# Router, second tile's transposes, gather and second gate's rows rearranged in a two-block transformer kernel

## The chip, the core and the metric

The kernel runs on one core of a Trainium2 chip. The core has TensorE (PE, matrix products into PSUM), VectorE (DVE), ScalarE (ACT), GpSimd (POOL) and SyncE (SP, which issues nearly all DMAs here). Each engine has its own instruction queue, and they meet only at semaphores. The metric is the device time of one execution in microseconds, the median over runs. A profiled execution gives one trace; its times are counted from the start of the span.

## What is computed

Two transformer blocks over 256 tokens of width 1024, all in float32. The first mixes tokens in two branches, normalises, and then sends each token to 4 of 32 experts. Only that part is touched by the change, together with the last gate of the second block:

```
h = layer_norm(ALPHA * x + mix, ln1_g, ln1_b)
logits = h @ router_w + router_b
top_vals, top_idx = lax.top_k(logits, 4)
gates = softmax(top_vals)
# for each chosen expert e of a token:
hcat = h @ w_up[e] + b_up[e]                  # 1024 x 2048
act = glu(hcat)                               # clipped, sigmoid(1.702 * x) gate
y_e = act @ w_down[e] + b_down[e]             # 1024 x 1024
out = sum over chosen e of gates[e] * y_e
# second block, at its end:
x = x + g1 * (mixed @ w_out)
x = x + g2 * ((silu(gt) * up) @ w_down)
```

`g1` and `g2` are rows of 1024 numbers that come out of `c @ w_ada`; every token uses the same row.

## The kernel before

The program is a row of blocks, `first_mix`, `branches`, `experts`, `second_mix`, `output`. Within a block each engine has a list of instructions in the order in which the code is written, and between blocks all engines meet at a barrier. The tokens are two tiles (t = 0, 1) of 128.

**Routing, the end of `branches`.** VectorE normalises a tile in two halves of 512 columns (L1125, L1127). TensorE turns each half (`turn`, L925, four transposes of 128x128 into one PSUM bank), ScalarE or VectorE copies it out to `hT` (tile name `fbuf_sgq`), and TensorE multiplies by the router's weights (`logits`, L936). Then for each tile VectorE's `top` adds the bias, takes the eight largest, finds their indices, converts these, compares them with 0..31 and sums the one-hots to `chosen` (L1132 to L1138). ScalarE takes the exponentials. TensorE adds up `chosen` over tokens (L993 to L997), which gives each token its place in each expert's list and the count of each expert. VectorE makes the gates (L1155 to L1158), the places (L1162, L1164) and, by `choose` (L860), the one-hot `sel` (tile name `keep_tri`) that picks up to 64 tokens for each of the first two experts. A `fill` is a matmul whose result nobody reads. `gate_rows` (L942) spreads g1 and g2 over all partitions by a product of ones with a diagonal matrix; ScalarE copies them to `gB`, which lies over the diagonals.

**Experts.** Each engine enters the block after the barrier. SyncE issues the load of the down biases (L1253, into `y`), reads the number of extra rounds that VectorE works out from the counts, and goes on to refill chunks. TensorE waits for `sel`, gathers the chosen tokens (L870, 32 matmul instructions), reads the rounds (L1244), waits for both bias loads (L1298, `bias_in`), enters two nested loops (L1366, L1367) and starts a pair of experts after a wait for `xg_ready`, which ScalarE gives after copying the gathered rows to `xg`. A pair is two experts in 12 chunks of 2 MB: up-weights (L1307), down-weights (L1332), transposes, a scatter-add (L1291), and the gather for the next pair. There are 16 pairs. VectorE chooses for the next pair inside the loop.

**Weights.** Nine chunks fit into memory. SyncE issues all nine during `branches`, as the space comes free, the last two (into `more`) after the last product with `w_out`. From then on each further chunk waits until TensorE has used one up:

```
for i in range(lo, hi):
    sp.wait_ge(used, done + 2 * (i - PLACES + 1))
    load_expert(k, sp, a, first, i)
```

`used` counts up by one for every 8 matmul instructions of weights, so the first refill waits for 16. All loads by SyncE go through one queue.

**Output block.** TensorE runs three fills (L2100) while VectorE normalises, then transposes and multiplies by `w_out`, `w_gu` and `w_down`; the last step on VectorE multiplies by g2 (L2317).

## Time and profile before

| | us |
|---|---|
| median of three runs | 1532.1 |
| lowest, highest run | 1530.8, 1532.8 |
| the profiled execution | 1531.5 |
| its span | 1529.6 |

| engine | busy us | share of the span |
|---|---|---|
| TensorE, matmuls | 1423.6 | 93% |
| TensorE, weight loads | 838.8 | 55% |
| VectorE | 591.9 | 39% |
| ScalarE | 444.9 | 29% |
| GpSimd | 39.1 | 3% |

The DMA engines moved 516 MB, on average 338 GB/s. A busy TensorE is not yet an engine at its limit: matmuls are pipelined and their ends are modelled. An idle time in a timeline stands in brackets, with what ended it. A wait for several semaphores is put down to the engine that came last. "issue" means that nothing the profile shows was waited for, and an engine's name with a q means its sequencer, which runs register steps, waits and branches. The granted clock (PEclk) is a share of 2.4 GHz.

### The profile page before, as it was taken

What the parts mean: (1) busy time and instruction counts of PE and PEld (TensorE: products, weight loads), DVE (VectorE), ACT (ScalarE), POOL (GpSimd) and SP (SyncE); (2) the same over time, 40 slices, a digit from 0 to 9 for tenths busy, and PEclk for the clock granted to TensorE, in tenths of its full rate; (3) what the DMA queues carried; (4) which work ended last, traced back from release to release, by engine and by line L of the source; (5) the groups of instructions that cost most, each with busy time, mean ns of one, the idle gap of its engine ahead of it and who ended that gap; (6) DMA issues with size and microseconds to landing.
All of it is one profiled execution on the core that took longest, in us unless ns stands there. A gap on an engine that the chain in (4) does not pass through costs nothing. (4 is left out here: it accounts for less than half of the span.)

```text
span 1529.6 us, 19821 instructions
## 1 busy us (share of the span) xinstructions
PE 1423.6 (93%) x7981; PEld 838.8 (55%) x7981; DVE 591.9 (39%) x1030; ACT 444.9 (29%) x577; POOL 39.1 (3%) x80
## 2 busy tenths in 40 slices
PE   8999999999999999988988988989988999899998
PEld 8988798344334434323423423323333788788887
DVE  4985447211210211210210210210211786677765
ACT  5654533121111112111111111111111536454343
POOL 2000030000000000000000000000000022000000
PEclk9999999999999999999999999999999999999999
DMA  9598999899999999999999999999999361345552
GB/s 283 171 299 272 327 334 397 361 426 429 427 428 428 428 428 428 429 428 428 429 428 429 428 429 428 429 428 429 428 427 382 104 191 56 99 150 193 192 187 88
DMA packets 126901, 516.46 MB, mean 338 GB/s; under 512 B 6869, under 2 KB 95294, under 8 KB 102238
## 3 DMA queue, kind: packets, MB, share of 16 engines
q1 hardware_dynamic: 126558, 514.64, 84.6%
q10 hardware_dynamic: 288, 1.05, 0.2%
q8 instruction: 39, 0.64, 0.2%
q14 instruction: 16, 0.13, 0.0%
HBM read 514.62 MB, written 1.05 MB: 337 GB/s over the span
## 5 line engine op out<-in xcount | busy, mean ns | idle before, releaser
L1307 PE MATMUL ps<-ring,xg 128*64 128x512 f32 x1456 | 324.8, 595 | 27.3 <-DMA ring<-in_expert_w_up 23.2
L1450 DVE TENSOR_TENSOR glu<-ps,bupT 128x512 f32<-128x512 f32 x32 | 22.1, 692 | 717.5 <-PE ps L1316 717.5
L1307 PEld LDWEIGHTS ps<-ring,xg 128*64 128x64 f32 x1456 | 101.7, 137 | 244.8 <-issue 186.2
L86 ACT ACTIVATE hrow<-ps 128x1024 f32<-128x1024 f32 x32 | 32.7, 1023 | 474.4 <-PE ps L1307 474.4
L1332 PE MATMUL ps<-ring,act 128*64 128x512 f32 x608 | 136.8, 597 | 1.2 <-ACT y L86 1.1
L2134 PE MATMUL ps<-h_halves,w_hi 128*128 128x512 f32 x352 | 123.1, 394 | 1.1 <-DVE h_halves L2287 1.1
L2236 DVE TENSOR_TENSOR w_lo<-ring,w_hi 128x2048 fp32r<-128x2048 f32 x36 | 82.5, 2291 | 61.2 <-ACT w_hi L86 61.2
L1307 PE MATMUL ps<-more,xg 128*64 128x512 f32 x416 | 93.1, 595 | 8.4 <-DMA more<-in_expert_w_up 7.2
L2136 PE MATMUL ps<-h_halves,w_lo 128*128 128x256 f32 x352 | 98.7, 280 | 0.0
L86 ACT ACTIVATE y<-ps 64x512 f32<-64x512 f32 x64 | 37.8, 591 | 182.8 <-PE ps L1332 182.5
L86 ACT ACTIVATE w_hi<-ring 128x2048 fp32r<-128x2048 f32 (+1 forms) x38 | 70.7, 1864 | 60.0 <-PE ps L2136 32.6
L86 ACT ACTIVATE in_hi<-ring 128x1024 fp32r<-128x1024 f32 (+1 forms) x72 | 72.4, 1043 | 52.2 <-DMA ring<-in_w_in 24.7
L1332 PEld LDWEIGHTS ps<-ring,act 128*64 128x64 f32 x608 | 41.5, 137 | 82.3 <-issue 72.5
L270 DVE TENSOR_TENSOR in_lo<-ring,in_hi 128x1024 fp32r<-128x1024 f32 x56 | 66.2, 1220 | 49.7 <-ACT in_hi L86 49.7
L538 PE MATMUL ps<-x_hi,in_hi 128*128 128x256 f32 x272 | 77.8, 286 | 0.0
L538 PE MATMUL ps<-x_lo,in_hi 128*128 128x256 f32 x272 | 76.0, 279 | 0.0
L538 PE MATMUL ps<-x_hi,in_lo 128*128 128x256 f32 x272 | 75.9, 279 | 0.0
L2134 PEld LDWEIGHTS ps<-h_halves,w_hi 128*128 128x128 f32 x352 | 66.0, 187 | 16.6 <-issue 1.3
L1316 PE MATMUL ps<-ident,hrow 128*128 128x128 f32 x256 | 36.5, 286 | 37.4 <-ACT hrow L86 37.4
L870 PE MATMUL ps<-keep_tri,h 128*128 128x128 f32 x544 | 67.3, 282 | 0.6 <-PEq L898 0.6
L1307 PEld LDWEIGHTS ps<-more,xg 128*64 128x64 f32 x416 | 28.9, 137 | 70.9 <-issue 51.8
L870 PEld LDWEIGHTS ps<-keep_tri,h 128*128 128x128 f32 x544 | 65.5, 196 | 3.0 <-issue 1.6
(409 smaller groups left out, 2218.1 us busy)
## 6 DMA issues: line engine op xcount, KB each, us to landing
ring<-in_expert_w_up SPq DMA_DIRECT2D x91, 2048.0 KB, 36.8
ring<-in_expert_w_down SPq DMA_DIRECT2D x38, 2048.0 KB, 39.3
more<-in_expert_w_up SPq DMA_DIRECT2D x26, 2048.0 KB, 35.5
more<-in_expert_w_down SPq DMA_DIRECT2D x16, 2048.0 KB, 38.8
ring<-in_w_in SPq DMA_DIRECT2D x29, 1024.0 KB, 9.0
ring<-in_w_ada SPq DMA_DIRECT2D x24, 1024.0 KB, 6.5
x_xT_xn<-in_expert_w_up SPq DMA_DIRECT2D x11, 2048.0 KB, 36.9
ring<-in_w_gu SPq DMA_DIRECT2D x22, 1024.0 KB, 5.1
```

Of the source, the lines that this page charges most:

```text
L86: return nc.scalar.activation(out, x, ACT.Copy)
L270: nc.vector.tensor_tensor(k.wlo1[:, n % 4, :], w[:, half * 1024:(half + 1) * 1024], k.whi1[:, n % 4, :].bitcast(F32), ALU.subtract).then_i ...
L538: last = nc.tensor.matmul(out, left, right, start=(j == 0 and kq == 0 and m == 0), stop=(j == 1 and kq == KD - 1 and m == 2), skip_group_c ...
L870: last = nc.tensor.matmul(out, k.h[:, t, (q // 2) * 256 + q % 2:(q // 2 + 1) * 256:2], k.sel[:, t, :], start=(t == 0), stop=(t == TT - 1))
L1307: last = nc.tensor.matmul(up[a2 * CAP:(a2 + 1) * CAP, u, :], k.xg[:, q, h * CAP:(h + 1) * CAP], w[:, c:c + 512], start=(q == 0), stop=(q = ...
L1316: last = nc.tensor.transpose(turned[:, par, j * P:(j + 1) * P], k.hrow[:, hidden_columns(j, par)], k.ident[:, :])
L1332: last = nc.tensor.matmul(down[a2 * CAP:(a2 + 1) * CAP, :], k.act[:, h, m % 4, m // 4, :], w[:, c:c + 512], start=(m == 0), stop=(m == KF ...
L1450: link(nc.vector.tensor_tensor(k.glu[:, :, :, :], g, b[:, 0].to_broadcast(wide), ALU.add))
L2134: nc.tensor.matmul(out, w[0][:, q, s], k.hh[:, q, :, :].rearrange("p v t -> p (v t)"), start=(i == 0), stop=False, skip_group_check=True)
L2136: last = nc.tensor.matmul(out[:, 0:T], w[1][:, q, s], k.hhi[:, q, :], start=False, stop=(i == KD - 1), skip_group_check=True)
L2236: nc.vector.tensor_tensor(k.wlo[i % 2][:, :], k.ring[:, LATE[i % len(LATE)], :], k.whi[i % 2][:, :].bitcast(F32), ALU.subtract).then_inc(w ...
```

## The change

The changes, in the order of the program:

- The slot numbers count from 1 (`iota`), so that a place is (position + 1) * chosen and 0 where a token isn't chosen; the subtraction of 1 goes.
- The second tile's transposes go half by half into two banks each. ScalarE copies the first two blocks of 128 of each half and VectorE the other two. The logits of the second tile are summed in pairs of blocks, the first of them before the tile's last transposes.
- `top`: the logits get four columns of 3e38 behind the 32, so the eight largest hold these four and the four chosen ones; a match-and-replace takes the eight out, and `chosen` is where something changed. The negated maximum, which ScalarE waits for, comes last.
- The rows of g1 are made in two parts, one between the tiles and one behind. The rows of g2 are made in the output block, in place of two of three fills, and ScalarE copies them there; TensorE waits for that copy before the third chunk of `w_out`.
- The counts of the experts go to a bank of their own, with a second `pos_done`, which VectorE waits for in the next block.
- `choose` without gates is one compare of 256 elements in place of four of 64, also inside the expert loop.
- The first half of the first gather stands in the routing block, in place of its last fill. All gathers are signalled by halves, ScalarE copies `xg` in halves, and the up-weights of a pair wait for the first half before block 0 and for the second before block 4.

The bias load, its wait and the places where the chunks are issued are as before.

TensorE, from the end of the routing block to the first expert's matmuls, before. `keep_tri` is `sel`, `ring` holds weights.

```order
L878 MATMUL ps<-h,ident 128x512
L898 UNCONDITIONAL_BRANCH
L1286 UNCONDITIONAL_BRANCH [waits barrier_Pool_Activation_PE_DVE_SP_release]
L870 MATMUL ps<-keep_tri,h 128x128 [waits hot_ready]
L870 MATMUL ps<-keep_tri,h 128x128 x15
L1244 TENSOR_LOAD rounds [waits rounds]
L1244 ISA x2
L1366 UNCONDITIONAL_BRANCH [waits bias_in]
L1367 UNCONDITIONAL_BRANCH
L1367 ISA
L1193 ISA [waits xg_ready]
```

The same place in the change:

```order
L875 MATMUL ps<-keep_tri,h 128x128 [waits hot_ready]
L875 MATMUL ps<-keep_tri,h 128x128 x7
L904 UNCONDITIONAL_BRANCH
L1290 UNCONDITIONAL_BRANCH [waits barrier_Pool_Activation_PE_DVE_SP_release]
L875 MATMUL ps<-keep_tri,h 128x128 x8
L1248 TENSOR_LOAD rounds [waits rounds]
L1248 ISA x2
L1371 UNCONDITIONAL_BRANCH [waits bias_in]
L1372 UNCONDITIONAL_BRANCH
L1372 ISA
L1197 ISA [waits xg_ready]
L1312 MATMUL ps<-ring,xg 64x512 [waits expert_in0]
```

Half of the gather now stands ahead of the barrier and the fill is gone; rounds, `bias_in`, loop entry and `xg_ready` follow in the same order.

VectorE, `top` of one tile, before (`m` is the eight largest, `ada_acc` the one-hot):

```order
L1132 TENSOR_TENSOR lg<-ps,rb 128x32 [waits logits_done]
L1133 MAX m<-lg 128x8 [waits chain_dve]
L1134 TENSOR_SCALAR small<-m 128x1 [waits chain_dve]
L1135 MAX_INDEX ix<-m,lg 128x8
L1136 CAST ixf<-ix 128x8 [waits chain_dve]
L1137 TENSOR_TENSOR ada_acc<-iota,ixf 128x128 [waits chain_dve]
L1138 TENSOR_REDUCE chosen<-ada_acc 128x32 [waits chain_dve]
```

and in the change:

```order
L1137 TENSOR_TENSOR lg<-ps,rb 128x32 [waits logits_done]
L1138 MAX m<-lg 128x8 [waits chain_dve]
L1139 MATCH_REPLACE rest_lg<-m,lg 128x36 [waits chain_dve]
L1140 TENSOR_TENSOR chosen<-rest_lg,lg 128x32 [waits chain_dve]
L1142 TENSOR_SCALAR small<-m 128x1
```

Seven instructions have become five. VectorE, from the positions to `sel`, before:

```order
L1162 SCALAR_TENSOR_TENSOR place<-ps,chosen 128x2x32 [waits pos_done]
L1164 TENSOR_SCALAR place<-place 128x2x32 [waits chain_dve]
L860 TENSOR_SCALAR keep_tri<-iota,place 128x64 [waits chain_dve]
```

and in the change:

```order
L1167 SCALAR_TENSOR_TENSOR place<-ps,chosen 128x2x32 [waits pos_done]
L859 TENSOR_TENSOR keep_tri<-iota,place 128x256 [waits chain_dve]
```

The subtraction and three of four compares (the row `x3` behind these) are gone.

The core of the diff:

```diff
-            link(nc.gpsimd.iota(k.iota_i[:, :], pattern=[[1, CAP]], base=0, channel_multiplier=0))
+            link(nc.gpsimd.iota(k.iota_i[:, :], pattern=[[1, CAP]], base=1, channel_multiplier=0))
...
+    if not gated:
+        both = [P, TT, 2, CAP]
+        return nc.vector.tensor_tensor(k.sel.rearrange("p t (h n) -> p t h n", h=2),
+                                       k.slots[:, :].unsqueeze(1).unsqueeze(1).to_broadcast(both),
+                                       k.place[:, :, bass.ds(p * 2, 2)].unsqueeze(3).to_broadcast(both), ALU.is_equal)
     for h in range(2):
         for t in range(TT):
             place = k.place[:, t, bass.ds(p * 2 + h, 1)]
-            g = (k.gate[:, t, bass.ds(p * 2 + h, 1)], ALU.mult) if gated else (None, ALU.bypass)
-            last = nc.vector.tensor_scalar((k.sel_gated if gated else k.sel)[:, t, h * CAP:(h + 1) * CAP], k.slots[:, :],
-                                           place, g[0], ALU.is_equal, g[1])
+            last = nc.vector.tensor_scalar(k.sel_gated[:, t, h * CAP:(h + 1) * CAP], k.slots[:, :], place,
+                                           k.gate[:, t, bass.ds(p * 2 + h, 1)], ALU.is_equal, ALU.mult)
...
-                    last = nc.tensor.transpose(k.ps[:, bank[t][half], j * P:(j + 1) * P],
+                    b, at = (bank[t][half], j) if t == 0 else (bank[t][half] + 4 * (j // 2), j % 2)
+                    last = nc.tensor.transpose(k.ps[:, b, at * P:(at + 1) * P],
...
-            logits(0)
-            gate_rows(0)
+            logits(0, range(4)).then_inc(log_done, 1)
+            gate_row(0)
             turn(1, 0)
+            logits(1, (0,))
             turn(1, 1)
-            logits(1)
-            gate_rows(1)
+            logits(1, (1, 2, 3)).then_inc(log_done, 1)
+            gate_row(1).then_inc(gb_done, 1)
             pe.wait_ge(m_ready, 2)
             mm = k.chosen
             nc.tensor.matmul(k.ps[:, 4, 0:E], k.strict[:, :], mm[:, 0, :], start=True, stop=True)
             nc.tensor.matmul(k.ps[:, 4, E:2 * E], k.ones[:, :], mm[:, 0, :], start=True, stop=False)
-            nc.tensor.matmul(k.ps[:, 4, E:2 * E], k.strict[:, :], mm[:, 1, :], start=False, stop=True)
-            nc.tensor.matmul(k.ps[:, 4, 2 * E:3 * E], k.ones[:, :], mm[:, 0, :], start=True, stop=False)
-            nc.tensor.matmul(k.ps[:, 4, 2 * E:3 * E], k.ones[:, :], mm[:, 1, :], start=False, stop=True)\
+            nc.tensor.matmul(k.ps[:, 4, E:2 * E], k.strict[:, :], mm[:, 1, :], start=False, stop=True)\
+                .then_inc(pos_done, 1)
+            nc.tensor.matmul(k.ps[:, 7, 0:E], k.ones[:, :], mm[:, 0, :], start=True, stop=False)
+            nc.tensor.matmul(k.ps[:, 7, 0:E], k.ones[:, :], mm[:, 1, :], start=False, stop=True)\
                 .then_inc(pos_done, 1)
             pe.wait_ge(gate_ready, 1)
             for t in range(TT):
-                last = nc.tensor.transpose(k.ps[0:E, 5, t * P:(t + 1) * P], k.gate[:, t, :], k.ident[:, :])
+                last = nc.tensor.transpose(k.ps[0:E, 6, t * P:(t + 1) * P], k.gate[:, t, :], k.ident[:, :])
             last.then_inc(gT_done, 1)
-            fill(nc, k, 3, k.h[:, 0, 0:512], 1)
+            pe.wait_ge(k.hot_ready, 1)
+            gather(nc, k, 5, range(4)).then_inc(k.g_done, 1)
...
-                if t == 0:
-                    evacuate(0, 1)
+                evacuate(t, 1)
             for t in range(TT):
                 act.wait_ge(negmax, t + 1)
-                nc.scalar.activation(ex[:, t, :], lg[:, t, :], ACT.Exp, bias=k.small[:, t:t + 1]).then_inc(expd, 1)
-            for n in range(2):
-                gate_copy(n)
+                nc.scalar.activation(ex[:, t, :], lg[:, t, 0:E], ACT.Exp, bias=k.small[:, t:t + 1]).then_inc(expd, 1)
+            act.wait_ge(gb_done, 1)
+            act_copy(nc, k.gB[:, 0, :], k.flat[:, 0:1024])
...
+            link(nc.vector.memset(lg[:, :, E:E + 4], LARGE))
...
-                link(nc.vector.tensor_tensor(lg[:, t, :], k.ps[:, 4 + t, 0:E], k.rb[:, :], ALU.add))
+                link(nc.vector.tensor_tensor(lg[:, t, 0:E], k.ps[:, 4 + t, 0:E], k.rb[:, :], ALU.add))
                 link(nc.vector.max(m8[:, t, :], lg[:, t, :]))
-                nc.vector.tensor_scalar(k.small[:, t:t + 1], m8[:, t, 0:1], -1.0, None, ALU.mult).then_inc(negmax, 1)
-                link(nc.vector.max_index(ix[:, t, :], m8[:, t, :], lg[:, t, :]))
-                link(nc.vector.tensor_copy(ixf[:, t, :], ix[:, t, :]))
-                link(nc.vector.tensor_tensor(one_hot[:, t], bc(k.iota[:, 0:E], 1, 4), bc(ixf[:, t, 0:4], 2, E), ALU.is_equal))
-                nc.vector.tensor_reduce(k.chosen[:, t, :], one_hot[:, t].rearrange("p j e -> p e j"), AX.X, ALU.add)\
+                link(nc.vector.match_replace(rest_lg[:, t, :], m8[:, t, :], lg[:, t, :], -LARGE))
+                nc.vector.tensor_tensor(k.chosen[:, t, :], rest_lg[:, t, 0:E], lg[:, t, 0:E], ALU.not_equal)\
                     .then_inc(m_ready, 1)
+                nc.vector.tensor_scalar(k.small[:, t:t + 1], m8[:, t, 4:5], -1.0, None, ALU.mult).then_inc(negmax, 1)
...
-            dve.wait_ge(hT_done, 4)
-            nc.vector.tensor_copy(hT[:, 4:8, P:T], k.ps[:, bank[1][1], :].rearrange("p (k n) -> p k n", k=4))\
-                .then_inc(hT_last, 1)
+            for half in range(2):
+                dve.wait_ge(hT_done, half + 3)
+                nc.vector.tensor_copy(hT[:, 4 * half + 2:4 * half + 4, P:T],
+                                      k.ps[:, bank[1][half] + 4, 0:2 * P].rearrange("p (k n) -> p k n", k=2))\
+                    .then_inc(hT_last, 1)
...
-            link(nc.vector.tensor_scalar(pl, pl, -1.0, None, ALU.add))
...
-            pe.wait_ge(hot_ready, 1)
-            gather(nc, k, 5, range(KD)).then_inc(g_done, 1)
+            gather(nc, k, 5, range(4, KD)).then_inc(g_done, 1)
             extra = extra_rounds(pe)
             pe.wait_ge(k.bias_in, 32)
             def up_weights(r, turn, at, n, h):
                 for q in range(KD):
+                    if h == 0 and q % 4 == 0:
+                        pe.wait_ge(xg_ready, n * 2 + q // 4 + 1)
...
-                pe.wait_ge(xg_ready, n + 1)
...
-                    gather(nc, k, 5, range(KD)).then_inc(g_done, 1)
+                    for half in range(2):
+                        gather(nc, k, 5, range(4 * half, 4 * half + 4)).then_inc(g_done, 1)
...
-            act.wait_ge(g_done, 1)
-            act_copy(nc, k.xg[:, :, :].rearrange("p k n -> p (k n)"), flat(rows)).then_inc(xg_ready, 1)
+            def gathered(n, src):
+                for half in range(2):
+                    act.wait_ge(g_done, n * 2 + half + 1)
+                    act_copy(nc, k.xg[:, 4 * half:4 * half + 4, :].rearrange("p k n -> p (k n)"), src[:, half, :])\
+                        .then_inc(xg_ready, 1)
+
+            gathered(0, rows)
...
+            dve.wait_ge(k.pos_done, 2)
+            start(nc.vector.tensor_reduce(k.small[:, 8:9], k.ps[:, 7, 0:E], AX.X, ALU.max))
...
-            fill(nc, k, 4, k.gB[:, 0, 0:512], 3)
+            for half in range(2):
+                last = nc.tensor.matmul(k.ps[:, 6 + half, :], k.ones[:, :], k.diag[1][:, half * 512:(half + 1) * 512],
+                                        start=True, stop=True)
+            last.then_inc(k.gb_done, 1)
+            fill(nc, k, 4, k.gB[:, 0, 0:512], 1)
             turned(mixed, mn, mt)
             for c in range(4):
                 w = chunk(L_OUT + c)
+                if c == 2:
+                    pe.wait_ge(g2_copied, 1)
...
+            act.wait_ge(k.gb_done, 2)
+            act_copy(nc, k.gB[:, 1, :], k.flat[:, 3072:4096]).then_inc(g2_copied, 1)
```

## Rows read from the trace of the kernel before

**Rows 1.** The page, the span in 40 slices: busy share of the DMA engines, tenths.
```profile
DMA  9598999899999999999999999999999361345552
```

**Rows 2.** Waits of TensorE, 300 to 1180 us: waiter, releaser: us, times, longest.
```profile
PE ps L1307 <- DMA ring<-in_expert_w_up: 23.2, 19, 1.2
```

**Rows 3.** Busy time by window: us, five engines with counts, PEclk, DMA share, GB/s.
```profile
266.00:267.00 1.00, 0.28 (x3) 0.09 (x1) 0.82 (x2) 0.69 (x1) 0.00 (x0) 1.00 0.09 29
267.00:272.50 5.50, 4.69 (x22) 1.69 (x24) 0.00 (x0) 3.16 (x4) 0.00 (x0) 1.00 0.00 0
...
276.00:1170.00 894.00, 817.52 (x3912) 321.98 (x3910) 173.98 (x353) 148.24 (x186) 0.00 (x0) 1.00 1.01 428
```

**Rows 4.** Timeline of SyncE's DMA issues: start, duration, line, transfer.
```profile
249.65 0.43 SPq L1218 DMA_DIRECT2D more<-in_expert_w_down  x1
262.22 0.33 SPq L1253 DMA_DIRECT2D y<-in_expert_b_down  x1
271.67 7.17 SPq L1218 DMA_DIRECT2D ring<-in_expert_w_down  x3
```

**Rows 5.** Timeline of TensorE, end of routing: start, duration, [idle before <-releaser].
```profile
259.32 0.41 PE L993 MATMUL ps<-chosen,strict 128*128 128x32 f32 x2 [0.21 <-DVE chosen L1138]
...
262.27 4.01 PE L870 MATMUL ps<-keep_tri,h 128*128 128x128 f32 x32 [0.57 <-PEq L898]
267.81 13.95 PE L1307 MATMUL ps<-ring,xg 128*64 128x512 f32 x64 [1.53 <-ACT xg L86]
```

**Rows 6.** Timeline of ScalarE: the copy of the gathered rows.
```profile
266.31 1.02 ACT L86 ACTIVATE xg<-ps 128x1024 f32<-128x1024 f32 x1 [5.07 <-PE ps L870]
```

**Rows 7.** Instructions of TensorE's sequencer by line: duration ns, first, last start.
```profile
L1244 PEldq SEQ_ASSERT  x1: 32/32/32, 264.8 to 264.8; - x1
...
L1366 PEldq MOVE  x2: 29/36/42, 267.2 to 267.2; - x2
...
L1193 PEldq FUSED_REGOPS  x1: 102/102/102, 267.6 to 267.6; - x1
```

**Rows 8.** Load into `y` (down biases): issue to landing.
```profile
DMA to landing us min/median/max: 4.9/4.9/4.9
```

**Rows 9.** Loads into `more`, issued at 249.28 and 249.65: issue to landing.
```profile
DMA to landing us min/median/max: 12.3/14.8/17.2
```

**Rows 10.** Timeline of VectorE: last copy, router, place, one-hot.
```profile
255.32 0.69 DVE L1149 COPY fbuf_sgq<-ps 128x512 f32<-128x512 f32 x1 [0.75 <-PE ps L925]
255.92 0.18 DVE L1132 TENSOR_TENSOR lg<-ps,rb 128x32 f32<-128x32 f32 x1
...
258.56 0.29 DVE L1137 TENSOR_TENSOR ada_acc<-iota,ixf 128x128 f32<-128x128 f32 x1
258.89 0.37 DVE L1138 TENSOR_REDUCE chosen<-ada_acc 128x32 f32<-128x128 f32 x1
...
260.66 0.23 DVE L1162 SCALAR_TENSOR_TENSOR place<-ps,chosen 128x64 f32<-128x64 f32 x1 [0.42 <-PE ps L997]
...
261.15 0.74 DVE L860 TENSOR_SCALAR keep_tri<-iota,place 128x64 f32<-128x64 f32 x4
```

**Rows 11.** Timelines of TensorE and ScalarE, start of the output block.
```profile
1302.93 2.81 PE L878 MATMUL ps<-x_xT_xn,ident 128*128 128x512 f32 x6 [1.50 <-PEq L1517]
...
1317.83 0.42 ACT L2196 ACTIVATE x_xT_xn<-h 128x256 f32<-128x256 f32 x1 [5.88 <-DVE h L2270]
```

**Rows 12.** Timeline of TensorE, start of the program.
```profile
8.76 1.97 PE L548 MATMUL ps<-ident,x_xT_xn 128*128 128x128 f32 x8 [2.20 <-DMA x_xT_xn<-in_x]
...
12.23 1.91 PE L518 MATMUL ps<-x_hi,in_lo 128*128 128x256 f32 x8
13.94 1.16 PE L518 MATMUL ps<-x_lo,in_hi 128*128 128x256 f32 x8
```

**Rows 13.** Busy time by window, end of the program; columns as in rows 3.
```profile
1525.70:1529.50 3.80, 0.07 (x1) 0.00 (x0) 1.49 (x3) 0.00 (x0) 0.00 (x0) 1.00 0.46 176
1529.50:1529.60 0.10, 0.00 (x0) 0.00 (x0) 0.00 (x0) 0.00 (x0) 0.00 (x0) 0.80 0.00 0
```

66 lines of the change are left out of this document (29 added, 37 removed).

## The prediction

> **What bounds the kernel now.** I read the slices of the page first. The DMA line is 9 in nearly every slice from about 270 us to 1170 us [rows 1]: this is the expert stage, which streams every expert's weights. The list of what TensorE waited for in that stage has the stream in it: 23.2 us in 19 waits for up-weights in the ring [rows 2]. The windows say how full the stream is: from 276 to 1170 us the 16 DMA engines are busy (1.01) at 428 GB/s, and from 267.0 to 272.5 us they do nothing at all [rows 3]. So the stage ends when a fixed number of bytes has passed, and it can end earlier only if the hole of 5.5 us in front of the stream gets smaller. TensorE's waits for weights show that it keeps nothing in reserve by the end, so I take one microsecond at the first refill as one microsecond at the end.
>
> What ends the hole? SyncE issued the last of the nine chunks that fit before the stage at 249.65, then the small load of the down biases at 262.22, and the first refill only at 271.67 [rows 4]. The refill waits until TensorE has used up one chunk, that is 16 matmuls into the expert loop, and the loop's first matmul began at 267.81 [rows 5]. So the question for this change is one only: **what let TensorE start at 267.81?**
>
> The obvious answer is the routing chain: choice, positions, one-hot, gather, then ScalarE's copy `xg`, from 266.31 for 1.02 us, so done at 267.33 [rows 6]. The sequencer's own rows say something else [rows 7]. It finished reading the number of rounds at 264.8 (SEQ_ASSERT, L1244). Its next instruction is the loop entry of L1366, which stands behind the wait for `bias_in` at L1298, and it ran at 267.2. Two more steps follow, and the register step of L1193, which carries the wait for `xg_ready`, ran at 267.6, about 0.3 us after `xg` was finished. The down biases were issued at 262.22 and landed 4.9 us later [rows 4, 8], at 267.12. That fits the 267.2. **TensorE waited for the bias load, not for routing.** `xg` came second, with 0.3 us to spare.
>
> Why 4.9 us for 128 KB? The load stands in SyncE's queue behind the chunk issued at 249.65, which landed 17.2 us after its issue [rows 4, 9], at 266.85. The biases are done 0.27 us after the data in front of them. Issuing them a little earlier or later would change nothing.
>
> **The change part by part.** The sum is made against the profiled execution, 1531.5 us (span 1529.6 and 1.9 around it), which lies 0.6 below the median 1532.1 of the three runs.
>
> *Second tile in two banks.* VectorE's copy of 512 columns took 0.69 us [rows 10]. It becomes two of 256 columns, one of them before the last transposes. Half a copy is about 0.42 with the fixed part, so the chain gets 0.25 shorter. One of the two gate-row pairs of matmuls also no longer stands before the second tile's transposes. But VectorE delivers that tile's second half only at 254.57 anyway (it then waits 0.75 for the transposes, [rows 10]), so I count nothing.
>
> *Router in fewer operations.* From the end of the copy (255.92) to the end of the second `chosen` (258.89 + 0.37) were 3.3 us for two tiles [rows 10], 1.63 each. The index search, cast, one-hot of 128 elements (0.29) and reduction (0.37) go. A match-and-replace and a compare over 32 elements come; the trace has no match-and-replace. Bounds: as cheap as a small operation (0.2) or as dear as the one-hot and reduction that it replaces (0.7). I take 0.3, since it reads as few elements as the index search. About 0.95 per tile is left, so `chosen` is ready 1.4 us earlier, with the copies 1.65.
>
> *Positions.* TensorE does six matmul instructions instead of ten before the first `pos_done`, the stretch from 259.32 on [rows 5], about 0.5 less. VectorE is still busy with the four gate operations then, so the place step, at 260.66 now, moves by 1.6 and not by 2.1.
>
> *Place and one-hot.* From the place step at 260.66 to the first compare at 261.15 are two small operations; the subtraction, half of that, goes (0.25). Four compares, 0.74 together, become one of 256 elements. It lies between 0.29 (128 elements) and 0.69 (512), at 0.42 [rows 10]. Together 0.5 us. `hot_ready` then comes at about 259.75 instead of 261.9.
>
> *Gather by halves.* The first 16 of 32 matmuls, about 2.0 of the 4.01 us [rows 5], run before the blocks change, from 259.85 to 261.85. All engines meet at the block's end, so TensorE's half sets that point, at about 262.1; it was 262.2. The second half ends near 264.2 (now 266.28), and the second half copy of `xg` near 264.9 (now 267.33). **Routing and gather are 2.1 to 2.4 us shorter.**
>
> *What is left of it at the start of the experts.* The order on TensorE is gather, rounds, `bias_in`, loop entry, `xg_ready`; the diff does not touch the wait or the load. The load is issued at 262.1 instead of 262.2 and still lies behind the chunks that land at 266.85. It lands at 267.1, and the loop begins 0.65 later, at 267.8: **0.0**. The 2.4 us turn into waiting. The cover works both ways: routing may be 2.3 us dearer than I think before it costs anything.
>
> *Inside the loop.* ScalarE copies `xg` twice (about 0.6 each) instead of once (1.02), VectorE makes one compare instead of four, TensorE has one more wait. The copy is needed one stretch of down-weights later, and the stage is held by the stream [rows 3]: 0. If that cover were gone it would be 0.2 us in each of 16 pairs, 3 us.
>
> *Second gate's rows.* TensorE replaces two of the three fill matmuls of the output block by the two gate-row matmuls of the same 512 columns [rows 11]. ScalarE gets a copy of 1.02 us there and has 5.88 us idle right behind it [rows 11]: 0. In the routing block its removed copy was off the path: 0.
>
> Sum: 0.0, from -0.3 to +0.3 for the spread of the landing. **Forecast 1532.1**, no difference that can be measured.
>
> **The rivals.** *The clock drops.* TensorE's idle time before the expert loop was 1.53 us [rows 5]. It becomes 267.8 - 264.25 = 3.55 us, since the gather ends earlier, the start does not, and the fill at the block's end is gone. The longest between two matmuls in this trace is 2.20 us, near its start [rows 12]; the 1.53 us left the clock at 1.00 [rows 3]. At the very end the granted clock fell (mean 0.80 in the last 0.1 us) some 3.8 us after the last matmul [rows 13]. 3.55 is less than 3.8, but not by much. Price: at the start of the program eight matmuls of 256 columns took 1.91 us at 12.23 and 1.16 at 13.94 [rows 12], so the lower of the two levels, 1.2 GHz, held for some 5.2 us from the restart at 8.76. The 16 matmuls up to the first refill take 3.45 us at 2.4 GHz (a quarter of the 13.95 for 64, [rows 5]). At half clock 12 of them fill the 5.2 us and 4 follow at full clock: 6.1, so 2.6 later, **1534.7**; if all 16 are slow 3.4, 1535.5. It decides once the idle time is long enough, and nothing gives it back, since the stream starts later. The Trainium skill, page TensorE: Matmul & The Clock Gate, section Why this matters for your kernels, advises against idle gaps of this kind, because the gate then returns to half clock. By that rule this case, with the 1534.7 worked out above, would be the one to expect; no idle time within this trace is long enough to agree or not.
>
> *The biases land earlier.* If the 4.9 us are a matter of issue and not of the queue in front, TensorE starts when `xg` is ready, at 265.2 instead of 267.8: **1529.5**. Against it speaks that both landings lie 0.27 apart [rows 8, 9]. The Trainium skill, page DMA: Bandwidth & Descriptors, gives a fixed cost of about 2 us to a transfer; by that the load would land at some 264.4, and the trace's 4.9 speaks for the queue.
>
> *The change doesn't do what it says.* If routing were over 2.3 us dearer (a match-and-replace or a wide compare of several us), the start would slip by the rest. No row is near that: about 1533.
>
> **How the numbers follow.** Forecast 0.70, clock 0.17, earlier landing 0.08, dearer routing or something unseen 0.05. The three runs spread from 1530.8 to 1532.8, so the forecast alone spans 1530.7 to 1533.5. The range reaches to 1535.0 for most of the clock case, and to 1530.2 below; the earlier landing is left out. A difference of 0.2%, 3.1 us, is about what a measurement can tell. Only the case of 16 slow matmuls passes it upwards (1535.5), which with the unseen gives slower 0.10. The earlier landing stays just within it (1529.5 is 0.17%), so faster has 0.07 and same 0.83.
>
> **What would show it.** Right: the gather's second half ends near 264.2; the loop entry runs at 267.2 again, straight after the biases' landing; the first expert matmul is at 267.8 and the first refill at 271.7; TensorE's idle time before it is about 3.5 us; the DMA hole is still 5.5 us. Wrong: a loop entry well before 267 (earlier landing), a granted clock under 1.00 behind 265 with the refill at 274 (clock), or a place step no earlier than 260.7 (routing).

## The result: slower, and most of it before the changed code begins

The two kernels, timed beside each other:

| | before | after |
|---|---|---|
| median of 8 executions each, us | 1533.0 (1530.8 to 1534.4) | 1536.1 (1535.1 to 1539.9) |
| ratio, 95% interval | | 1.0027 [1.0016, 1.0038] |
| span of the profiled execution, us | 1529.6 | 1533.3 |
| mean granted clock in it | 1.000 | 0.998 |

Forecast: 1532.1, no measurable difference, range up to 1535.0. The changed kernel is slower, by 3.1 us in the medians and by 4.1 us by the ratio. A second comparison (after_again, below) gave 1.0040 [1.0027, 1.0053]. All of this is far under 2%; "slower" means here that the interval lies above 1.

The timeline of TensorE in the changed kernel: the end of the first stage, routing, the entry to the expert loop. Columns as in [rows 5].

```profile
251.51 0.28 PE L973 MATMUL ps<-in_hi,x_lo 128*128 128x256 f32 x1
251.63 1.04 PE L932 MATMUL ps<-ident,h 128*128 128x128 f32 x8
...
262.59 2.15 PE L875 MATMUL ps<-keep_tri,h 128*128 128x128 f32 x16 [0.20 <-DVE keep_tri L859]
265.07 2.12 PE L875 MATMUL ps<-keep_tri,h 128*128 128x128 f32 x16 [0.33 <-PEq L904]
269.80 6.64 PE L1312 MATMUL ps<-ring,xg 128*64 128x512 f32 x22 [2.61 <-DMA y<-in_expert_b_down]
```

And the two rows of the kernel before that answer to the first two:

```profile
248.97 0.28 PE L968 MATMUL ps<-in_hi,x_lo 128*128 128x256 f32 x1
249.09 0.38 PE L925 MATMUL ps<-ident,h 128*128 128x128 f32 x2
```

Three things stand in these rows. **The transposes that begin the routing block start 2.54 us late** (251.63 against 249.09), and everything ahead of them is code that the diff leaves alone. **The expert loop starts 2.0 us late** (269.80 against 267.81 in [rows 5]), so routing gained something, and its idle time is now put down to the bias load. **That idle time is 2.61 us, against 1.53.**

VectorE in routing, with the new operations:

```profile
257.02 0.42 DVE L1153 COPY fbuf_sgq<-ps 128x256 f32<-128x256 f32 x1
257.99 0.42 DVE L1153 COPY fbuf_sgq<-ps 128x256 f32<-128x256 f32 x1 [0.54 <-PE ps L932]
258.33 0.18 DVE L1137 TENSOR_TENSOR lg<-ps,rb 128x32 f32<-128x32 f32 x1
...
258.85 0.18 DVE L1139 MATCH_REPLACE8 rest_lg<-m,lg 128x36 f32<-128x36 f32 x1
259.07 0.19 DVE L1140 TENSOR_TENSOR chosen<-rest_lg,lg 128x32 f32<-128x32 f32 x1
...
261.00 0.22 DVE L1160 TENSOR_TENSOR ex<-ex,chosen 128x64 f32<-128x64 f32 x1 [0.46 <-ACT ex L1044]
...
261.86 0.22 DVE L1167 SCALAR_TENSOR_TENSOR place<-ps,chosen 128x64 f32<-128x64 f32 x1
262.11 0.43 DVE L859 TENSOR_TENSOR keep_tri<-iota,place 128x256 f32<-128x256 f32 x1
```

The match-and-replace takes 0.18 us, the wide compare 0.43. A new wait of 0.46 for ScalarE's exponentials stands ahead of the gate operations; the faster choice has caught up with them.

SyncE's issues, and how long the two loads ahead of the expert loop took from issue to landing (`y`, then `more`):

```profile
252.20 0.43 SPq L1222 DMA_DIRECT2D more<-in_expert_w_down  x1
265.01 0.33 SPq L1257 DMA_DIRECT2D y<-in_expert_b_down  x1
275.36 7.17 SPq L1222 DMA_DIRECT2D ring<-in_expert_w_down  x3
```
```profile
DMA to landing us min/median/max: 4.1/4.1/4.1
```
```profile
DMA to landing us min/median/max: 11.6/14.2/16.7
```

Biases: 265.01 + 4.1 = 269.11. The last chunk in front of them: 252.20 + 16.7 = 268.90. The loop entry of TensorE's sequencer stands at 269.13:

```profile
L1371 PEldq MOVE  x2: 33/38/42, 269.1 to 269.2; - x2
```

That is the pattern of [rows 7 to 9] once more. The first refill comes at 275.36, 5.56 us after the loop's start; before it was 3.86 ([rows 4, 5]). The windows tell why (us; PE, PEld, DVE, ACT, POOL busy; PEclk; DMA share; GB/s):

```profile
266.00:268.50 2.50, 1.19 (x11) 1.00 (x9) 2.00 (x3) 1.10 (x2) 0.00 (x0) 1.00 0.42 144
268.50:269.50 1.00, 0.00 (x0) 0.00 (x0) 1.00 (x2) 0.99 (x2) 0.00 (x0) 1.00 0.00 0
269.50:270.00 0.50, 0.20 (x2) 0.20 (x4) 0.12 (x1) 0.48 (x2) 0.00 (x0) 1.00 0.00 0
270.00:271.00 1.00, 1.00 (x4) 0.25 (x2) 0.00 (x0) 0.85 (x1) 0.00 (x0) 0.63 0.00 0
271.00:272.00 1.00, 1.00 (x5) 0.26 (x3) 0.00 (x0) 0.00 (x0) 0.00 (x0) 0.50 0.00 0
272.00:273.00 1.00, 1.00 (x6) 0.40 (x4) 0.00 (x0) 0.00 (x0) 0.00 (x0) 0.50 0.00 0
273.00:274.00 1.00, 1.00 (x6) 0.25 (x4) 0.00 (x0) 0.00 (x0) 0.00 (x0) 0.67 0.00 0
274.00:275.00 1.00, 1.00 (x8) 0.32 (x6) 0.00 (x0) 0.00 (x0) 0.00 (x0) 1.00 0.00 0
```

The granted clock falls to 0.50, that is 1.2 GHz, just after TensorE has started again, and comes back near 273.7, 3.4 us later. The first 64 matmuls of the loop take 15.65 us instead of 13.95 [rows 5], 1.7 more, which is half of those 3.4 us. So the difference builds up like this, each number being after minus before at the same instruction: +2.54 at the first transposes, +2.0 at the loop's start, +3.7 at the first refill, +4.4 at the output stage's start (1310.35 to 1314.74), +3.6 at the end. The refill's 3.7 us arrives at the end, as the forecast had it. The fit to 0.1 us is partly luck: from the first refill to the end the kernel before took 1258.0 us in its first trace and 1257.1 in its second.

### The profile page after: what moved, and what is told of

It reads as the page before. It is cut to its first block and busy times, and to the rows that moved or that the text cites. A ratio compares the mean times of both kernels' runs of the same rounds, so it can differ in the third digit from the quotient of the medians.

```text
span 1533.3 us, 19774 instructions
## 1 busy us (share of the span) xinstructions
PE 1425.7 (93%) x7975; PEld 843.2 (55%) x7975; DVE 584.9 (38%) x976; ACT 448.0 (29%) x595; POOL 38.9 (3%) x80
## 5 line engine op out<-in xcount | busy, mean ns | idle before, releaser
L2147 PEld LDWEIGHTS ps<-h_halves,w_hi 128*128 128x128 f32 x352 | 66.0, 187 | 16.7 <-issue 1.3
L1321 PEld LDWEIGHTS ps<-ident,hrow 128*128 128x128 f32 x256 | 31.0, 194 | 66.1 <-issue 66.1
```

What stands on the lines that cost most here:

```text
L1321: last = nc.tensor.transpose(turned[:, par, j * P:(j + 1) * P], k.hrow[:, hidden_columns(j, par)], k.ident[:, :])
L2147: nc.tensor.matmul(out, w[0][:, q, s], k.hh[:, q, :, :].rearrange("p v t -> p (v t)"), start=(i == 0), stop=False, skip_group_check=True)
```

## Experiments

All ratios are to the kernel before, run on the same chip in the same comparison.

**The kernel before once more** (no edit).

> The kernel before, unchanged, for a second trace of it. Two readings of the changed kernel's trace are to be told apart. In it everything up to the last transposes of the first tile is already 2.5 us late (251.63 against 249.09), in code that the change hardly touches. If that is the spread of the first stage between executions, this trace differs from the first trace of before by one to three us at the same place, its granted clock stays at 1.00 and its time lies between 1530.8 and 1534.4. If the first stage is really slower in the changed kernel, this trace repeats 249.1 within 0.3.

1529.4 us, span 1527.6. Its routing block began 1.3 us earlier, and it had a drop of the clock at 1301.8, where the first trace had none. Most of the 1.3 us stems from the program's start: the first product begins at the same time (10.34 us, before 10.38), but its second eight matmuls took 1.10 us, from 11.91, and not 1.91 [rows 12], so TensorE left its slow level sooner. Of my two readings the first fits the place, a first stage that varies by 1 to 3 us; but the time lies under the range that I gave and the clock didn't stay at 1.00. And since the stage came earlier and not later, the run doesn't explain the +2.54 us. Two traces of one kernel differ by 2 us, and stages have to be compared by their own length.

**The wait for the biases moved behind the loop entry**, in the changed kernel (a_bias_late) and in the kernel before (b_bias_late):

```diff
-            pe.wait_ge(k.bias_in, 32)
...
             def scatter():
+                pe.wait_ge(k.bias_in, 32)
                 for t, out in enumerate(scat):
```

> The changed kernel with the wait for the bias loads taken from ahead of the expert loop and put ahead of each scatter, which is the first reader of the biases. Theory: TensorE idles 2.6 us for the bias load and the clock drops in that time. Then the first expert matmul moves from 269.8 to about 267.5 (behind the gather's end at 267.2), the idle time falls under 0.6 us, the granted clock stays at 1.00 there, and the first refill moves from 275.4 to 271.3, 4 us earlier: 1531 to 1532.5, ratio to before 0.998 to 0.9995. Rival, the loss comes from the first stage or from the expert loop itself (one more wait for each pair, xg in two copies): the start moves, but the time stays at 1535 or above.

> The same move of the wait in the kernel before. In its trace the bias load was done 0.3 us before xg mattered, so the first expert matmul can move only from 267.8 to about 267.6. Theory: within 0.3 us of before, ratio 0.9995 to 1.0005, clock 1.00. Rival, the wait costs more than that in most executions of before and the trace was a lucky one: faster by 1 us or more.

a_bias_late: 1534.1, ratio 1.0003 [0.9990, 1.0016]. b_bias_late: 1532.0, 0.9991 [0.9979, 1.0003]. In a_bias_late the idle time ahead of the loop shrinks from 2.61 to the 0.32 us of a loop entry:

```profile
262.37 2.15 PE L875 MATMUL ps<-keep_tri,h 128*128 128x128 f32 x16 [0.20 <-DVE keep_tri L859]
264.85 2.12 PE L875 MATMUL ps<-keep_tri,h 128*128 128x128 f32 x16 [0.33 <-PEq L904]
267.29 7.09 PE L1312 MATMUL ps<-ring,xg 128*64 128x512 f32 x32 [0.32 <-issue]
```

There is no drop, and the first refill stands at 271.15 instead of 275.36; the span is 4.5 us shorter (1528.8 against 1533.3). The wait for the biases was the binding one, and in the changed kernel's trace it costs the clock too. The timed ratio missed what I expected (0.998 to 0.9995), and the trace is nearly the fastest of its 12 runs: their mean granted clock was 0.9973, that of the kernel before in the same comparison 0.9981. So in most runs the clock fell somewhere else, and of the 4.5 us only 2.0 show in the median. In the kernel before little is to be had, since `xg` came 0.3 us behind.

**Work put into the gap instead** (a_fill_gap): three 128x512 matmuls between the gather and the loop.

```diff
             gather(nc, k, 5, range(4, KD)).then_inc(g_done, 1)
+            fill(nc, k, 3, k.h[:, 0, 0:512], 3)
```

> The changed kernel with three fill matmuls of 512 columns (2.6 us, nobody reads them) between the gather's second half and the bias wait. Theory of the clock: the idle time ahead of the expert loop shrinks from 2.6 us to about 0.2, TensorE stays at 2.4 GHz, the start stays at 269.8 and the 16 matmuls before the first refill take 3.5 us instead of 5.2, so the time falls by 1.6 us to about 1534.5 and the mean granted clock rises by 0.001. Rival, the clock's drop there costs nothing: the time stays at 1536 within 0.5.

1535.4 (I had 1534.5), 1.0013 [1.0002, 1.0025]. The mean granted clock of its runs was 0.9982, that of the changed kernel's, in the first comparison, 0.9976. The gap is gone and there is no drop behind it, but the trace has one of 6.8 us inside the routing block:

```profile
257.00:258.00 1.00, 0.89 (x10) 0.78 (x8) 0.88 (x5) 0.93 (x2) 0.00 (x0) 1.00 0.96 410
259.00:265.00 6.00, 6.00 (x27) 5.28 (x26) 2.10 (x12) 1.78 (x4) 0.00 (x0) 0.50 1.02 429
266.00:267.00 1.00, 0.84 (x7) 0.88 (x8) 0.74 (x6) 0.60 (x1) 0.00 (x0) 1.00 0.16 66
```

That drop begins at 258.7, ahead of the edit, so the edit didn't bring it; the loop starts at 270.79. Filling the gap is no cure by itself, and the routing block has a weakness of its own (below).

**Where do the 2.54 us ahead of routing come from?** They grow steadily from 30 us on, so it isn't one event. The groups of the page show that the same matmuls take 3 to 4 ns more each (line, operation, count, busy us, mean ns of one; idle), first before, then after:

```profile
L538 PE MATMUL ps<-x_hi,in_hi 128*128 128x256 f32 x272 | 77.8, 286 | 0.0
L538 PE MATMUL ps<-x_lo,in_hi 128*128 128x256 f32 x272 | 76.0, 279 | 0.0
```
```profile
L539 PE MATMUL ps<-x_hi,in_hi 128*128 128x256 f32 x272 | 78.7, 289 | 0.0
L539 PE MATMUL ps<-x_lo,in_hi 128*128 128x256 f32 x272 | 76.9, 283 | 0.0
```

The last 286 steps of the stage, which nothing interrupts, give the pitch, the time from one start to the next: from 215.29 to 248.97 before, 33.68 us, 117.8 ns each; from 217.20 to 251.51 after, 34.31 us, 120.0 ns. The change replaces small tiles (`ixf`, `ix`, `lg`) by others that are 192 bytes longer in all, and the tiles allocated behind them move: `x_hi` from byte 179744 of a partition to 179936, `x_lo` with it, while the weights `in_hi` and `in_lo` come from the other end and stay. Five kernels change the addresses alone, with an unused tile ahead of `x_hi`, or of `in_hi`:

```diff
+                k.pad = half("pad", [P, N])
                 k.xhi, k.xlo = (half(n, [P, KD, T]) for n in ("x_hi", "x_lo"))
```

N is 16 in a_x_back, 48 in b_x_shift, 16 in b_x_64, 64 in b_x_256; a_in_shift has 48 ahead of `in_hi` instead.

> The changed kernel with one unused tile of 64 bytes per partition ahead of x_hi and x_lo, the activation halves of the first stage. The change had moved these two from byte 179744 to 179936 of a partition; they now start at 180000. Theory A (where the operands lie sets the pitch of the first stage's matmuls: 117.5 ns in every trace of the old layout, 120 ns in every trace of the new one, whatever else was edited): the remainder of the address by 256 is again 32 as in the kernel before, so the pitch of the 128x256 matmuls before 250 us is 117 to 118 ns, the first transpose of the routing block starts within 0.6 us of where it stands in the kernel before (249.1 us, or its offset at the program's start added), and the time falls by about 2.5 us against the changed kernel, to a ratio of 1.0005 to 1.0020. Rival B (the pitch comes from something else that the change edited in the program, for example the blocks' code or the semaphores): the pitch stays at 120 ns, the routing block starts 2.5 us late, ratio 1.0027 as for the changed kernel.

> The kernel before with one unused tile of 192 bytes per partition ahead of x_hi and x_lo, and nothing else: they start at byte 179936, where the change puts them. Theory A (the addresses): the pitch of the 128x256 matmuls before 250 us goes from 117.5 to 120 ns, the routing block starts 2.5 us later than in the kernel before, and the time rises by 2 to 3 us, ratio 1.0013 to 1.0020. Rival B (something else in the change): pitch 117 to 118 ns, ratio 0.9995 to 1.0005.

> The changed kernel with x_hi and x_lo left at byte 179936 (remainder 224 by 256) and the weight halves in_hi and in_lo moved down by 192 bytes, from 212960 to 212768 and from 196576 to 196384 (remainder 224 to 32). It tells a rule on the activations' own address from a rule on the two operands' distance. If the distance counts (the two operands slow each other where both have the same remainder): the pitch of the 128x256 matmuls before 250 us is 117 to 118 ns again. If the activations' own address counts: it stays at 120 ns. If weights at remainder 224 were what is slow: 117 to 118 ns too, and the kernel before, with weights at 224 and pitch 117.5, speaks against that already. One look: the time tells little, 1530 to 1538 us.

> The kernel before with an unused tile of 256 bytes ahead of x_hi and x_lo: they start at byte 180000, the place they have in the changed kernel with the 64 byte tile, whose first stage ran at 113 to 114 ns a matmul in one stretch and was 1.9 us shorter than in the kernel before. Theory A (a rule of the remainder alone: 32 against the weights' 224 by 256 is free of conflict): pitch 113 to 118 ns, never 120, the first stage as in the kernel before or up to 2 us shorter, ratio 0.9985 to 1.0005. Rival (any shift of x_hi costs, and the gain seen belongs to the changed program): pitch 120 ns and ratio 1.0013 to 1.0020. It also gives the fair partner for the changed kernel with its address restored.

> The kernel before with 64 bytes ahead of x_hi and x_lo: byte 179808, remainder 96 by 256, weights at 224. The slow layout has both operands at remainder 224, the two free ones 32 against 224 and 224 against 32. One distance, 128 bytes, tells two rules apart. If operands conflict when their remainders by 256 are equal: 117 to 118 ns or less before 250 us. If they conflict when their remainders by 128 are equal (96 and 96 here): 120 ns.

| kernel | remainder by 256: `x_hi`, `in_hi` | last 286 steps, us | ns each | ratio |
|---|---|---|---|---|
| before | 32, 224 | 33.68 | 117.8 | |
| b_x_256 | 32, 224 | 33.68 | 117.8 | 1.0001 [0.9991, 1.0010] |
| b_x_64 | 96, 224 | 34.32 | 120.0 | one run |
| b_x_shift | 224, 224 | 34.31 | 120.0 | 1.0005 [0.9995, 1.0016] |
| after | 224, 224 | 34.31 | 120.0 | 1.0027 [1.0016, 1.0038] |
| a_x_back | 32, 224 | 32.92 | 115.1 | 1.0011 [0.9998, 1.0023] |
| a_in_shift | 224, 32 | 33.69 | 117.8 | one run |

The first and last rows of that stretch in b_x_shift, which differs from the kernel before by 192 unused bytes:

```profile
218.91 0.28 PE L956 MATMUL ps<-x_lo,in_hi 128*128 128x256 f32 x1
...
253.22 0.28 PE L968 MATMUL ps<-in_hi,x_lo 128*128 128x256 f32 x1
```

and in a_in_shift, where `x_hi` stays where the change put it and the weights move:

```profile
216.72 0.28 PE L961 MATMUL ps<-x_lo,in_hi 128*128 128x256 f32 x1
...
250.41 0.28 PE L973 MATMUL ps<-in_hi,x_lo 128*128 128x256 f32 x1
```

So in this stage it isn't the address of one tile but of both: 120.0 ns where both have the same remainder, 113.3 to 117.8 where not. b_x_64 has remainders equal by 128 only; its last stretch is as slow, an earlier one (up to 52 us) lies between, at 118.6. My expectation for that kernel named both rules; the rule by 128 holds better. The traces settle the pitch. In a_x_back the last stretch ran at 115.1 ns, faster than the 117 to 118 that I expected, and routing began at 247.24, 1.85 us ahead of the kernel before and not within 0.6 of it. The timed ratios are blunter: a_x_back lies where it was expected, but its interval takes in 1.000; b_x_shift was expected at 1.0013 to 1.0020, and that was missed: its interval takes in 1.000 too and only reaches 1.0016. Its 12 runs had a mean clock of 0.9988, the kernel before 0.9983, which may hide a part. That the addresses alone cost time from start to end is thus shown in the traces and not in this ratio.

**Both costs out** (a_x_back_late): a_x_back with the later bias wait.

> The changed kernel with both suspected costs taken out: the 64 byte tile ahead of x_hi and x_lo, and TensorE's wait for the bias loads moved from the entry of the expert loop to the first scatter. If the two causes are separate and add up (address 2.5 us; idle ahead of the expert loop and the clock's drop behind it 2 us, the changed kernel having measured 1.0027): ratio 0.9975 to 0.9995, the fastest kernel so far, expert loop started before 268 us and no clock drop at 270 us. If the two are one cause or the saved time is waited out again further on: ratio 1.000 to 1.0015.

1531.1, **0.9976 [0.9964, 0.9988]**, at the lower edge of what was expected: the two add up. The mean clock rose from a_x_back's 0.9969 to 0.9979. Of a_x_back the trace shows what the later wait is worth, since there the forecast's own situation came about, the first stage not being late:

```profile
266.73 7.50 PE L1312 MATMUL ps<-ring,xg 128*64 128x512 f32 x26 [3.92 <-DMA y<-in_expert_b_down]
```
```profile
262.80:266.70 3.90, 0.00 (x1) 0.00 (x0) 2.21 (x3) 3.42 (x4) 0.00 (x0) 1.00 0.36 126
266.70:267.70 1.00, 0.97 (x6) 0.42 (x8) 0.00 (x0) 0.00 (x0) 0.00 (x0) 1.00 0.00 0
267.70:271.20 3.50, 3.50 (x12) 1.11 (x10) 0.00 (x0) 0.00 (x0) 0.00 (x0) 0.51 0.00 0
```

Idle 3.92 us (I had 3.55), then half clock from 267.8. But a_x_back_late has a 6.8 us drop as well, from 255.0, in routing.

**The thinner routing block** (a_late_filled): a_x_back_late with two 128x512 matmuls where the second gate's rows were.

```diff
             gate_row(0)
+            fill(nc, k, 1, k.h[:, 0, 0:512], 1)
...
+            fill(nc, k, 1, k.h[:, 0, 0:512], 1)
             gate_row(1).then_inc(gb_done, 1)
```

> The changed kernel with 64 bytes ahead of x_hi, the bias wait at the first scatter, and two extra 128x512 matmuls in the routing block where the kernel before had the second gate's rows. Question: three of six traces with the changed routing block show the granted clock at half for 6.8 us within it or right from its start (255.0, 258.5 and 258.7 us), none of the four traces with the routing block of before. If the thinner matmul work of the changed block brings that drop: none between 250 and 265 us here, mean clock over its runs above the 0.998 of the same kernel without them, ratio 0.9960 to 0.9974. If the drop has nothing to do with it: the same share of drops, and the added work costs 0 to 0.9 us: ratio 0.9976 to 0.9982.

1530.1 over six runs, 0.9977 [0.9964, 0.9989], no drop in its trace. What TensorE did in the block: busy 12.09 of 13 us before, 9.62 of 11 after.

```profile
249.00:262.00 13.00, 12.09 (x73) 8.27 (x71) 10.35 (x36) 6.10 (x10) 0.00 (x0) 1.00 1.00 426
```
```profile
251.60:262.60 11.00, 9.62 (x67) 7.20 (x65) 8.60 (x29) 5.16 (x10) 0.00 (x0) 1.00 1.01 427
```

Over all traces of the study a drop lies within routing in 4 of the 8 with the thinner block and in 0 of the 10 with the block of before or with the two matmuls put back. That speaks for it, but it is not shown. Drops of 3.4 or 6.8 us also stand between 111 and 116 us in three traces and between 1183 and 1201 in three, in code that both kernels share. And the ratio came out where I had put it for the case that the drop has nothing to do with the thinner block (0.9976 to 0.9982): the matmuls cost 0.9 us in the block, and the drops that they might avoid come only sometimes. The mean clock was 0.9988 against 0.9979, but of six runs.

**Operands apart in two later stages too** (a_second_shift): a_x_back_late with 64 bytes ahead of `in2_hi` and 64 ahead of `h_halves`.

```diff
+            k.pad2 = ht("pad2", [P, 16])
             k.whi2, k.wlo2 = (ht(n, [P, 3, 1024], R32) for n in ("in2_hi", "in2_lo"))
...
+            k.pad3 = lt("pad3", [P, 16])
             k.hh = lt("h_halves", [P, KD, 2, T], R32)
```

> The changed kernel with 64 bytes ahead of x_hi, the bias wait at the first scatter, and the same 64 byte step put between operands in two later stages: ahead of the second mixer's weight halves in2_hi and in2_lo (both operands had remainder 128; now 128 against 192) and ahead of h_halves in the output stage (128 against 192). Theory A (the conflict is a matter of the operands' places in every stage): the 128x256 matmuls of 1200 to 1290 and of 1310 to 1340 us go from 120 to 113 to 118 ns, some 1.5 to 3 us less in all, ratio 0.9955 to 0.9970, against 0.9976 for the same kernel without these two steps. Rival (120 ns there has another reason, for example the order of the passes): the pitch stays 120 ns and the ratio 0.9970 to 0.9985.

1531.7, 0.9980 [0.9971, 0.9989], not better; my 0.9955 to 0.9970 was missed. The second mixer's matmuls did get shorter (pitch 117 instead of 120 ns), and so did the first product of the output stage (`w_lo` with `h_halves`, mean 276 ns instead of 283). The last product's got longer: the groups from 1465 us on, changed kernel, then this one.

```profile
L2051 PE MATMUL ps<-w_hi,mlp_hi 128*128 128x512 f32 x88 | 34.3, 390 | 0.0
```
```profile
L2051 PE MATMUL ps<-w_hi,mlp_hi 128*128 128x512 f32 x88 | 34.8, 396 | 0.0
```

The step ahead of `h_halves` had also moved `mlp_hi` and `mlp_lo` against the weights: 264 matmuls, 6 ns each, 1.6 us. This goes against the rule: here both operands had remainder 128 in the faster layout, and 128 against 192 in the slower. So equal remainders are no general rule; what these 128x512 matmuls want was not tried, and a layout has to be measured stage by stage.

**Does the idle time itself bring the drop?** (b_idle): the kernel before with ScalarE's copy of the gathered rows made twice.

```diff
+            act_copy(nc, k.hrow[:, :], flat(rows))
             act_copy(nc, k.xg[:, :, :].rearrange("p k n -> p (k n)"), flat(rows)).then_inc(xg_ready, 1)
```

> The kernel before with ScalarE's copy of the gathered rows made twice, the first time into a tile that is not in use yet, so that the real copy and the expert loop come about 1 us later and TensorE idles about 2.5 us ahead of the first expert matmul instead of 1.53. Everything up to the gather's end stands as in the kernel before. Theory A (the idle time brings the clock's drop): the trace shows half clock for 3.4 us starting between 268 and 272 us, the first 64 expert matmuls take 15 to 16 us instead of 13.95, and the time is 1 to 2.7 us longer: ratio 1.0007 to 1.0018, mean clock of its runs below the 0.9983 of the kernel before. Rival B (the drop belongs to the changed routing block): no drop there, 64 matmuls in 13.9 to 14.1 us, ratio 1.0000 to 1.0007.

```profile
268.30 6.21 PE L1307 MATMUL ps<-ring,xg 128*64 128x512 f32 x20 [2.17 <-ACT xg L86]
```
```profile
266.00:268.50 2.50, 0.33 (x4) 0.20 (x4) 0.67 (x2) 2.31 (x3) 0.00 (x0) 1.00 0.02 7
268.50:269.50 1.00, 1.00 (x6) 0.39 (x4) 0.00 (x0) 0.99 (x2) 0.00 (x0) 0.85 0.00 0
269.50:270.00 0.50, 0.50 (x2) 0.00 (x0) 0.00 (x0) 0.48 (x2) 0.00 (x0) 0.50 0.00 0
```
```profile
273.87 3.74 SPq L1218 DMA_DIRECT2D ring<-in_expert_w_down  x2
```

Idle 2.17 us, half clock from 269.2, the refill 5.57 us after the start instead of 3.86: the old program shows the drop once its idle time is longer, and its first 64 matmuls take 15.65 us, as in the changed kernel. Over all 18 traces the drop at this place followed the idle times of 2.17, 2.51, 2.61 and 3.92 us, and none of the others (0.32 to 1.59 us, and the filled gap). The timed ratio, 1.0002 [0.9988, 1.0015], decides nothing: it allows both what I expected and no cost at all. Nor does the mean clock of the runs show the drop (0.9981, the kernel before 0.9982 beside it), so how often it comes, and what it costs over many executions, is not shown.

**Best of both programs** (a_best, b_best): a_late_filled, and the kernel before with the later bias wait, each with the 64 bytes ahead of `in2_hi`. **The changed kernel again** (after_again).

> The changed kernel with 64 bytes ahead of x_hi, the bias wait at the first scatter, the two fill products in the routing block, and 64 bytes ahead of in2_hi and in2_lo (not ahead of h_halves, where that step made the last 64 us of the output stage 1.5 us longer). In the layout where the second mixer's operands were apart its stage was 1.2 to 2 us shorter. If these add up: ratio 0.9955 to 0.9970, the fastest kernel of the study, no clock drop between 250 and 275 us. If the second mixer's gain is waited out elsewhere: 0.9970 to 0.9985.

> The kernel before with the bias wait at the first scatter and 64 bytes ahead of in2_hi and in2_lo; its x_hi is in a free place already. Against a_best it shows what the change is worth once nothing stands in its way: if the shorter routing (16.8 us from the first transpose to the first expert matmul, against 18.5 us) reaches the end, b_best is 1.3 to 2 us slower than a_best, ratio 0.9970 to 0.9985; if the refills of the ring, which start with the expert loop, are what counts and they are not ahead, both come out within 0.7 us of each other.

> The changed kernel unchanged, for a second profile and more executions. If the pitch of 120 ns is the layout's, it stands in this trace too, and the routing block starts 2.0 to 3.5 us later than in the kernel before. If the idle time of 2.6 us brings the drop, a drop of 3.4 us or more again stands between 250 and 275 us. Ratio 1.0020 to 1.0035.

a_best 1529.0, **0.9971 [0.9961, 0.9982]**; b_best 1531.1, 0.9990 [0.9979, 1.0002]; after_again 1.0040 [1.0027, 1.0053]. All three lie outside the ranges for my favoured cases (a_best just above 0.9970, b_best above 0.9985, after_again above 1.0035). In after_again's trace both costs stand again, with 120.0 ns, 2.51 us of idle time ahead of the loop and the drop at 270.2. The second mixer's groups, changed kernel and a_best:

```profile
L1558 PE MATMUL ps<-h_hi,in_lo 128*128 128x256 f32 x48 | 13.6, 283 | 0.0
```
```profile
L1560 PE MATMUL ps<-h_hi,in_lo 128*128 128x256 f32 x48 | 13.3, 276 | 0.0
```

a_best is faster than the kernel before and than the changed one. Its first refill comes 20.6 us after the first transposes (269.09 - 248.46), in b_best 22.3 (272.22 - 249.90): with nothing in its way the change is worth 1.7 us there. The medians lie 2.1 apart, but the two intervals overlap a little, and the two kernels differ ahead of routing too (last stretch 115.0 ns in a_best, 117.8 in b_best), so the 2.1 us are not the change's alone.

## Why the prediction was wrong, step by step

- *Durations.* Right. The copies took 0.42 each, the choice 0.93 per tile (258.33 to 259.26; I had 0.95), the match-and-replace 0.18 (0.3), place and one-hot 0.68 instead of 1.23 (0.55 less; I had 0.5). The place step came 1.3 us earlier against the block's start and not 1.6, because of the wait for the exponentials, which I had not counted.
- *Gather by halves.* Right in kind, about 0.5 us too hopeful: against the block's start its end came 1.6 us earlier (267.19 - 2.54 = 264.65 against 266.28) and the last `xg` copy ended 2.0 us earlier (267.83 - 2.54 = 265.29 against 267.33); I had 2.1 and 2.4.
- *What is left at the start of the experts.* The mechanism was right: the loop entry stands 0.02 us behind the biases' landing, which is 0.2 behind the chunk in front. The term was 0.0; it was -0.5, since the chunk landed 16.7 us after its issue and not 17.2 [rows 9], and the biases behind it. The a_bias_late run takes this wait away, and the gain shows.
- *Idle time and clock.* **This is the first step that failed.** I took 3.8 us, from the end of the program, as the idle time that matters, and let the clock case have 0.17. The idle times that led to a drop there were 2.17 to 3.92 us. The 2.20 us near the start, which I used, came before the engine had been at full clock (the eight transposes behind it took 1.97 us, against 1.04 in the routing block) and could say nothing. The price was right in kind and too high: 5.56 - 3.86 = 1.7 us, where I had 2.6. I took the low stretch to be 5.2 us, from the start of the program; it was 3.4 us, and half of that is lost. (A quarter of 13.95 is 3.49 and not 3.45, which changes nothing.) The Trainium skill, page TensorE: Matmul & The Clock Gate, section Why this matters for your kernels, warns of idle gaps between bursts; the traces here agree, and at gaps shorter than I had allowed for.
- *Everything ahead of the routing block.* **The second step, and the larger: it had no term in the sum.** I took it as unchanged because the diff doesn't touch it, and never asked what a changed list of tiles does to the addresses of the others. +2.54 us, all of it in code that the diff doesn't touch. Of 1296 matmuls of this kind in the stage, 2.2 ns each would be 2.9; part lies beside other waits.
- *Inside the loop, second gate's rows.* Right within what can be seen: from the first refill to the output stage the difference went from 3.7 to 4.4, and traces of the old program differ by as much there (1038.7 and 1038.9 us in the kernel before, 1039.3 and 1039.4 in b_bias_late and b_x_256, which leave that stretch alone). The gate rows in the output block delayed nothing: 4.4 stood at its start already. What they left behind, a thinner routing block, was not in the forecast at all.
- *Refill to end one for one.* Right, as well as two traces can tell: +3.7 at the refill, +3.6 at the end; in a_bias_late 4.2 us less at the refill and 4.5 less at the end.

The sum by these steps: 2.5 (operands) - 0.5 (landing) + 1.7 (clock) = 3.7, which is what the two traces differ by. The medians of the two comparisons differ by 3.1 and 5.1. With these two terms the forecast's mechanism gives the traces and the first comparison. The second one's interval begins at 1.0027, or 4.1 us, so a part of it stays open; its runs had a mean clock of 0.9970 against 0.9982, which speaks for drops that its one trace doesn't show.

## What to carry to other kernels

A change to the list of tiles is a change to every tile allocated behind it. Print the addresses of the matmuls' two operands before and after, and compare the mean duration of matmuls that the diff doesn't touch before looking at anything else. And when a wait takes the place of the work ahead of it, the wait is not free even if it ends at the same time: look at how long TensorE then idles and at the granted clock behind it, and move the wait to where its data is needed.

## What the runs showed of the hardware

- The pitch of back-to-back 128x256 matmuls (float32r tiles) in the first stage depended on where in a partition both operands lie relative to each other: 119.5 to 120.0 ns in each uninterrupted stretch with equal remainders by 256 (after, after_again, a_bias_late, a_fill_gap, b_x_shift; 120 in the second mixer's old layout, both at 128), 118.5 to 120.0 with remainders equal by 128 only (b_x_64), 113.3 to 117.8 with unequal ones. The 128x512 matmuls of the last stage did the opposite: mean duration 390 ns with equal remainders, 396 with unequal ones. In a_x_back the same layout as before gave 117.8 in most of the stage and 115.1 in its last stretch; what picks between these levels stays open. The Trainium skill, page TensorE: Matmul & The Clock Gate, section Step-by-step: what each phase is for, says that loading weights takes no SBUF bandwidth from the running matmul, the two having ports of their own. The measurement doesn't refute the ports, but the placement did cost 2% of the pitch (120.0 against 117.8 ns).
- The clock fell after 2.17 us without a matmul, ahead of the expert loop. It fell too behind the 1.50 us gap ahead of the output stage in 10 of 18 traces, of both kernels (in the changed kernel's from 1307.9 on), and in the others not there; and it did not fall behind a gap of 2.19 us at 1185.7 in a_fill_gap. So the length of the gap alone doesn't decide, and a trace without a drop is not proof that the place is safe.
- The output stage took 154.3, 155.2 or 156.6 us from its first to its last `h_halves` matmul in traces of the same code and addresses without a drop inside it (154.3 in a_x_back, 155.2 in a_late_filled, 156.6 in a_x_back_late). Its cause wasn't tried. It sets how well one trace's end can be compared with another's.
